# A two-layer Conformer and retention backbone: its opening by channel instead of by token

## The reference

```
mod_x = silu(c) @ ada_w[0] + ada_b[0]          # 6 * 1024 values: shift, scale, gate, twice
mod_c = silu(c_ctx) @ ada_w[0] + ada_b[0]      # the same for the context tokens
h = x * rsqrt(mean(x * x) + eps) * norm1_g     # RMSNorm of each token
h = h * (1 + scale) + shift
z = h @ pw1_w + pw1_b                          # 1024 -> 2048
u = a * sigmoid(g)                             # a, g: the halves of z
u = dwconv(u), 31 taps along the tokens
```

## Time and profile before

| | us |
|---|---|
| median of 3 runs | 1671.44 |
| lowest, highest | 1670.82, 1672.15 |
| the profiled execution | 1671.6 |
| its span | 1669.7 |
| TensorE, matmuls busy | 1641.5 (98%) |
| VectorE busy | 958.0 (57%) |
| ScalarE busy | 677.3 (41%) |
| GpSimd busy | 168.6 (10%) |

### The profile page before, as it was taken

One profiled execution on the slowest core, in us unless ns is written; L12 is line 12 of the kernel. 1 busy time (PEld: TensorE's weight loads), 2 busy tenths in 40 slices (PEclk: granted clock), 3 DMA queues, 4 the chain that ended last, 5 costly groups with the idle time before them and its releaser, 6 DMA issues.

```text
span 1669.7 us, 25661 instructions
## 1 busy us (share of the span) xinstructions
PE 1641.5 (98%) x10040; PEld 1435.3 (86%) x10040; DVE 958.0 (57%) x1511; ACT 677.3 (41%) x1019; POOL 168.6 (10%) x180
## 2 busy tenths in 40 slices
PE   6999989999999999999999999999999999999998
PEld 4777758998888888888899999999999888888888
DVE  6899987763424342334358665656566754543445
ACT  4656667542323222223245333424244543332333
POOL 1488851000000000000000000000000000000000
PEclk9999999999999999999999999999999999999999
DMA  9767742221221212121112121212112323232321
GB/s 338 254 251 251 252 160 95 75 76 48 67 76 56 70 60 67 55 71 57 57 51 92 64 70 39 83 51 63 58 64 76 99 81 123 89 101 89 100 88 51
DMA packets 58062, 165.64 MB, mean 99 GB/s; under 512 B 5288, under 2 KB 7192, under 8 KB 57976
## 3 DMA queue, kind: packets, MB, share of 16 engines
q1 hardware_dynamic: 54120, 150.43, 27.1%
q0 software_dynamic: 2992, 10.88, 2.0%
q10 hardware_dynamic: 864, 3.15, 0.5%
HBM read 162.34 MB, written 2.10 MB: 98 GB/s over the span
## 4 chain that ended last, share of the span: by engine, by line
PE 82%; DVE 14%; ACT 3%; issue 1%; DMA 0%; ACTq 0%; DVEq 0%
PE ps L674 81%; DVE ps L1867 3%; DVE ps L1884 3%; DVE w_lo L1663 2%; DVE rstd L1669 1%; DVE H_lo L1704 1%; PE ps L879 0%; DVE tmp L1692 0%; DVE ps L1882 0%; ACT sq L1251 0%; DVE sq L1692 0%; DVE rstd L1680 0%; ACT tmp L1251 0%; ACT H_hi L1242 0%; DVE ps L1864 0%
## 5 line engine op out<-in xcount | busy, mean ns | idle before, releaser
L674 PE MATMUL ps<-H_hi,w_hi 128*128 128x512 f32 (+1 forms) x1712 | 583.3, 341 | 8.4 <-DVE H_lo L1766 5.1
L674 PE MATMUL ps<-H_lo,w_hi 128*128 128x512 f32 (+1 forms) x1712 | 578.8, 338 | 0.0
L674 PE MATMUL ps<-H_hi,w_lo 128*128 128x512 f32 (+1 forms) x1712 | 578.1, 338 | 0.0
L674 PEld LDWEIGHTS ps<-H_hi,w_hi 128*128 128x128 f32 x1712 | 324.7, 190 | 62.2 <-issue 24.4
L674 PEld LDWEIGHTS ps<-H_hi,w_lo 128*128 128x128 f32 x1712 | 324.8, 190 | 35.0
L674 PEld LDWEIGHTS ps<-H_lo,w_hi 128*128 128x128 f32 x1712 | 324.9, 190 | 34.3
L1663 DVE TENSOR_TENSOR w_lo<-w_raw,w_hi 128x1024 fp32r<-128x1024 f32 x208 | 255.0, 1238 | 107.9 <-ACT w_hi L1204 75.0
L674 PE MATMUL ps<-mid_hi,w_hi 128*128 128x512 f32 (+1 forms) x592 | 199.4, 337 | 0.6
L674 PE MATMUL ps<-mid_lo,w_hi 128*128 128x512 f32 (+1 forms) x592 | 198.4, 335 | 0.0
L674 PE MATMUL ps<-mid_hi,w_lo 128*128 128x512 f32 (+1 forms) x592 | 198.0, 335 | 0.0
L2200 DVE SCALAR_TENSOR_TENSOR tmp<-ps,par,tmp 128x511 f32<-128x511 f32 x66 | 41.6, 658 | 231.3 <-ACT tmp L1548 155.1
(11 more groups left out here) (278 smaller groups left out, 2097.0 us busy)
## 6 DMA issues: line engine op xcount, KB each, us to landing
w_raw<-in_w_units SPq DMA_DIRECT2D x190, 512.0 KB, 3.5
ada<-in_ada_w SPq DMA_DIRECT2D x40, 1024.0 KB, 6.4
w_raw<-in_w_units SPq DMA_DIRECT2D x16, 384.0 KB, 3.3
ada<-in_ada_w POOLq DMA_DIRECT2D x4, 1024.0 KB, 13.1
conv<-in_x ACTq DMA_DIRECT2D x4, 512.0 KB, 5.6
ada_more<-in_ada_w POOLq DMA_DIRECT2D x2, 1024.0 KB, 14.6
conv<-in_ctx ACTq DMA_DIRECT2D x2, 512.0 KB, 9.4
w_raw<-in_w_units POOLq DMA_DIRECT2D x2, 512.0 KB, 18.5
```

What stands on the lines that cost most here:

```text
L674: return nc.tensor.matmul(o, a, b, start=first, stop=last, skip_group_check=True)
```

## The change

The inputs are laid out otherwise on the host (a permutation of the same numbers; no arithmetic): x and the context by channel (`x_cols`), all parameters as one table of 128 rows (`params`), ada_w in groups of contiguous 8 KB per partition (`ada_groups`). In the first layer the columns of the first four groups are interleaved, so that group m carries shift and scale of tiles 2m and 2m+1.

SP loads the parameters, x in four pieces of two tiles, and the identity. The token and parameter transposes and their copies are gone. ScalarE squares each tile, VectorE adds the eight squares (seven adds), and TensorE sums over the partitions with six one-column products. A root of one element, whose result nobody reads, stands before the real one. `keep_busy(n)` makes n products of mean_of with itself into a PSUM bank that is not read: 40 before the sums, 4 behind them, 10 behind the transposes of group 0. The constant group, the modulation and the tiles go by twos, and TensorE's steps alternate between gate and value. Unit 1 is loaded before group 2 instead of behind it.

```diff
-S_XT = 0
-S_PW1 = S_XT + 12
+S_PW1 = 0
...
-FIRST_GROUPS = [0, 2, 1, 3]
+FIRST_GROUPS = 4
...
+        tok_sums = ps[:, 5, 0:6]
+        x_squares = conv[:, KT - 1, 0:TOK]
...
+        def first_shift(j):
+            return 4 * (j // 2) + j % 2
...
+        def x_square(k):
+            return conv[:, k, 0:TOK] if k < KT - 1 else norm_buf[0]
...
-            rows = slice(half * D // 2, (half + 1) * D // 2)
-            g = FIRST_GROUPS[m]
-            eng.dma_start(ada_first[m][half], ada_w[0][rows, g * GROUP * P:(g + 1) * GROUP * P]
-                          .rearrange("(k p) n -> p k n", p=P)).then_inc(ada_first_in[m], 16)
+            eng.dma_start(ada_first[m][half], ada_groups[m, half].rearrange("p (k n) -> p k n", n=GROUP * P)) \
+                .then_inc(ada_first_in[m], 16)
...
-            for n, (lo, rows, src) in enumerate([
-                    (C_COL, 8, c.rearrange("b (t p) -> (b t) p", p=P)),
...
-                r0 = lo % P
-                sp.dma_start(prow[r0:r0 + rows, lo // P, :], src).then_inc(par_rows if lo < DW_W else tap_rows, 16)
-                if n == 0:
-                    sp.dma_start(ident[:], eye).then_inc(eye_in, 16)
+            sp.dma_start(par[:], params).then_inc(par_in, 16)
+            for n in range(KT // 2):
+                sp.dma_start(X[:, 2 * n:2 * n + 2, :], x_cols[:, 2 * n:2 * n + 2, :]).then_inc(x_in[n], 16)
+            sp.dma_start(ident[:], eye).then_inc(eye_in, 16)
...
-            pool.wait_ge(tokens_in[0], 32)
+            pool.wait_ge(x_in[1], 16)
...
             for m in range(2):
                 for half in range(2):
                     load_first(pool, m, half)
-            load_gate_or_value(0)
+                load_gate_or_value(m)
             for half in range(2):
                 load_first(pool, 2, half)
-            load_gate_or_value(1)
...
-            def token_transposes(t):
-                pe.wait_ge(tokens_in[t], 32)
...
-            pe.wait_ge(eye_in, 16)
-            token_transposes(0)
-            token_transposes(1)
...
-            pe.wait_ge(par_rows, 16 * 12)
-            par_transposes([(0, 128), (1, 116)], 6)
-            token_transposes(2)
-            pe.wait_ge(silu_c_ready, 2)
-            pe.wait_ge(par_ready, 1)
-            ada_products(0)
-            pe.wait_ge(tap_rows, 16 * 4)
-            par_transposes([(2, 128), (3, 120), (4, 66), (5, 66)], 1)
-            ada_transposes(0)
-            pe.wait_ge(filled, 4)
+            def keep_busy(n):
+                for _ in range(n):
+                    mm(ps[:, 2, 0:P], mean_of[:], mean_of[:], True, True)
+            pe.wait_ge(filled, 1)
+            keep_busy(40)
+            pe.wait_ge(x_added, KT - 1)
+            for t in range(6):
+                m = mm(tok_sums[:, t:t + 1], x_squares[:, t * P:(t + 1) * P], mean_of[:, 0:1], True, True)
+            m.then_inc(x_summed, 1)
+            keep_busy(4)
             pe.wait_ge(diag_ready, 1)
-            pe.wait_ge(slot_read[1], S_PW1 // 2)
             mm(ps[:, 3, :], mean_of[:], flat_sq[:, LATS], True, True)
             mm(ps[:, 4, 0:CTX], mean_of[:], flat_sq[:, CTXS], True, True).then_inc(rows_ready, 1)
-            ada_products(1)
-            ada_transposes(1)
+            pe.wait_ge(silu_c_ready, 2)
+            ada_products(0)
+            pe.wait_ge(eye_in, 16)
+            ada_transposes(0)
+            keep_busy(10)
...
-            for p in range(2):
-                pe.wait_ge(slot_read[p], S_PW1 // 2)
-            first_block(0, 0, 1)
+            ada_products(1)
+            ada_transposes(1)
+            first_block(0, 0, 2)
             ada_products(2)
-            first_block(0, 1, 3)
+            first_block(1, 0, 2)
             ada_transposes(2)
-            first_block(0, 3, 4)
-            pe.wait_ge(par_ready, 2)
+            first_block(0, 2, 4)
             ada_products(3)
-            first_block(1, 0, 1)
+            first_block(1, 2, 3)
             ada_transposes(3)
-            first_block(1, 1, 4)
-            first_block(0, KT // 2, KT - 2)
+            first_block(1, 3, 4)
+            first_block(0, 4, 6)
+            first_block(1, 4, 6)
+            first_block(0, 6, KT)
             ada_products(4)
-            first_block(0, KT - 2, KT)
-            first_block(1, KT // 2, KT)
+            first_block(1, 6, KT)
             ada_transposes(4)
             ada_products(5)
...
-            for t in range(LT):
-                act.dma_start(xin[:, t, :], x[0, t * P:(t + 1) * P, :]).then_inc(tokens_in[t // 2], 16)
...
-            for s in range(S_PW1):
-                t, jj = s // 4, s % 4
...
-            act.wait_ge(tok_var, 2)
-            A(tok_rstd[:], tok_mv[:, :, 1], ACT.Sqrt, bias=eps[:, 0:1]).then_inc(tok_std, 1)
-            ada_copy(0)
-            ada_copy(1)
-            split_hi(0, 0)
+            act.wait_ge(par_in, 16)
+            for v in range(2):
+                A(silu_c[:, :, v], par[:, C_COL + 8 * v:C_COL + 8 * v + 8], ACT.Silu).then_inc(silu_c_ready, 1)
+            for k in range(KT):
+                act.wait_ge(x_in[k // 2], 16)
+                A(x_square(k), X[:, k, :], ACT.Square).then_inc(x_squared, 1)
+            A(tok_std_row, eps[:, 0:1], ACT.Sqrt)
+            act.wait_ge(x_summed, 1)
+            A(tok_rstd[:], tok_sums, ACT.Sqrt, bias=eps[:, 0:1]).then_inc(tok_std, 1)
             def first_hi(j):
...
-                act.wait_ge(mod_ready, 2 if j < KT // 2 else 4)
+                act.wait_ge(mod_ready, 2 * (j // 2) + 2)
...
-            for j in range(KT // 2):
-                first_hi(j)
-            split_hi(1, 1)
-            ada_copy(2)
-            ada_copy(3)
-            for j in range(KT // 2, KT):
-                first_hi(j)
-                if j in (4, 6):
-                    split_hi(j // 2, j // 2)
+            for m in range(FIRST_GROUPS):
+                if m < 2:
+                    split_hi(m, m)
+                ada_copy(m)
+                for j in (2 * m, 2 * m + 1):
+                    first_hi(j)
+            split_hi(2, 2)
+            split_hi(3, 3)
             ada_copy(4)
...
-            def first_modulation(m, half):
-                dve.wait_ge(mod_sum, m)
-                js = slice(half * GROUP, (half + 1) * GROUP)
+            def first_modulation(m):
+                dve.wait_ge(mod_sum, m + 1)
+                js = slice(2 * m, 2 * m + 2)
                 rows = par[:, ADA_B:ADA_B + 2 * KT].rearrange("p (a j) -> p a j", a=2)[:, :, js]
-                cols = mod[:, 0, 0:2 * KT, :].rearrange("p (a j) c -> p a j c", a=2)[:, :, js, :]
-                v.tensor_tensor(cols, cols, rows.unsqueeze(3).to_broadcast([P, 2, GROUP, 2]), ALU.add).then_inc(mod_ready, 1)
-                dve.wait_ge(mod_ready, 2 * half + 1)
-                v.scalar_tensor_tensor(gain[:, 0, 0, js, :], mod[:, 0, KT + half * GROUP:KT + (half + 1) * GROUP, :], 1.0,
-                                       two(par[:, NORM1 + half * GROUP:NORM1 + (half + 1) * GROUP]), ALU.add, ALU.mult) \
+                cols = mod[:, 0, 4 * m:4 * m + 4, :].rearrange("p (a j) c -> p a j c", a=2)
+                v.tensor_tensor(cols, cols, rows.unsqueeze(3).to_broadcast([P, 2, 2, 2]), ALU.add).then_inc(mod_ready, 1)
+                dve.wait_ge(mod_ready, 2 * m + 1)
+                v.scalar_tensor_tensor(gain[:, 0, 0, js, :], mod[:, 0, 4 * m + 2:4 * m + 4, :], 1.0,
+                                       two(par[:, NORM1 + 2 * m:NORM1 + 2 * m + 2]), ALU.add, ALU.mult) \
                     .then_inc(mod_ready, 1)
-                dve.wait_ge(mod_ready, 2 * half + 2)
+                dve.wait_ge(mod_ready, 2 * m + 2)
...
-            for t in range(6):
-                if t % 2 == 0:
...
+            for k in range(1, KT):
+                dve.wait_ge(x_squared, k + 1)
+                if k > 1:
+                    dve.wait_ge(x_added, k - 1)
+                v.tensor_tensor(x_squares, x_square(0) if k == 1 else x_squares, x_square(k), ALU.add) \
+                    .then_inc(x_added, 1)
+            dve.wait_ge(par_in, 16)
             dve.wait_ge(tok_std, 1)
...
-            dve.wait_ge(par_T, 2)
-            v.tensor_copy(par[:, 256:504], ps[:, 1, 0:248])
-            for layer in range(DEPTH):
-                o = v.tensor_copy(par[:, FFN_DW_W + P * layer:FFN_DW_W + P * layer + 66],
-                                  ps[:, 1, 256 + P * layer:256 + P * layer + 66])
-            o.then_inc(par_ready, 1)
-            ada_sum(0, 0, FIRST_GROUPS[0])
-            for p in range(2):
-                dve.wait_ge(slot_read[p], S_PW1 // 2)
             dve.wait_ge(rows_ready, 1)
             def normed_rows(js):
@@ -1816,20 +1750,19 @@
                     v.tensor_tensor(xn(j), X[:, j, :], rstd_rows, ALU.mult).then_inc(xn_ready, 1)
                 dve.wait_ge(xn_ready, js[-1] + 1)
-            normed_rows(range(KT // 2))
-            dve.wait_ge(par_ready, 2)
-            ada_sum(1, 0, FIRST_GROUPS[1])
-            first_modulation(2, 0)
-            first_shifted(0)
```

(29 more changed lines are left out.)

110 lines of the change are left out of this document (31 added, 79 removed).

## The result

The changed kernel takes **1673.79 us** (median of 20 runs, 1670.83 to 1677.72), the kernel before beside it 1671.21 (20 runs, 1670.33 to 1672.15): ratio 1.0014, 95% interval 1.0008 to 1.0020. It is 2.6 us slower where 4.1 us faster was forecast, and outside the range of 1665.3 to 1670.6. The profiled execution took 1672.88, its span is 1671.1; in the kernel before these were 1671.6 and 1669.7.

What follows compares the result with a forecast made beforehand. VectorE's convolution taps bound the kernel, so only its start on block 0 counts: 20.8 + 32.6 = 53.4 instead of 57.53, 4.1 us earlier, giving 1667.3 us against the median of 1671.44; range 1665.3 to 1670.6.

Steps and rivals of the forecast that it cites:

- Part 1: Opening up to VectorE's first normalising product: loading x by channel and summing squares brings it 3.5 us earlier.
- R: Start of VectorE's first normalising product in the opening: forecast at 20.8 us instead of 24.29.
- the rival with the low clock: Opening on TensorE: low clock doubles sums (+1.2 us) and wide products (+1.5), or order costs waits; 1669.5 us, chance 0.16.
- The rival in which POOL's loads share the engines: Opening loads: x shares DMA engines with POOL's, lands at 14.7 us, gain 2.0, time 1669.4; chance 0.15.
- The slower rival: Opening on TensorE: 40 constant products never raise the clock, take 20 us and delay the sums; 1677.8 us, chance 0.07.
- Part 2: From R to block 0's gates: new order takes 32.6 us against 33.24 before.
- The interleaving: Gate and value steps alternating by twos, from R to block 0's gates: by itself gives only 0.6 us.
- The first step that failed: End of the opening on ScalarE: block 0's sigmoid, with its table load, fits between R+29 and R+31.4, hidden.
- B0: VectorE's start of gate times value on block 0: forecast at R + 32.6, 53.4 us instead of 57.53.
- The step that decides: Behind the opening: later stages keep whatever VectorE's start on block 0 gains, 4.1 us.
- the forecast's own last sign of being wrong: From block 0 through the convolution: a shift at 57 us that is gone by the convolution's end would refute the forecast.
- a group that lands 3 us late: Opening, ada weight loads: late landing cuts the gain to 1.4 to 2.9 us, 1669.5; shared chance 0.16.

Runs made afterwards that it cites:

- e1: Changed kernel with block 0's sigmoid ahead of ScalarE's copy of group 4; 1672.98 us, ratio 1.0011.
- e10c: e9c with 50 constant products ahead of the sums and 8 behind them, in place of 54 and 4; 1668.86 us, ratio 0.9989.
- e3: Changed kernel with 20 more constant products ahead of the products of group 5; 1672.69 us, ratio 1.0011.
- e5: Changed kernel with 54 constant products ahead of the sums in place of 40; 1672.54 us, ratio 1.0006.
- e6: Changed kernel with 54 constant products ahead of the sums and group 4's products two k-steps earlier; 1670.44 us, ratio 0.9994.
- e9c: e7 with one constant sigmoid behind ScalarE's copy of group 4, loading the table ahead; 1670.05 us, ratio 0.9992.
- e7: e6 plus 12 constant products ahead of the LayerNorm's sums and 8 ahead of the second pointwise convolution; 1669.64 us, ratio 0.9992.
- e8: Kernel before the change, with only group 4's products moved late, to where the change put them; 1676.59 us, ratio 1.0031.

## Why the prediction was wrong

*Part 1 was right in its chain, and in its number partly by luck.* R was forecast at 20.8 (the terms as written add up to 20.7) and came at 20.97. The last piece of x ended ScalarE's last wait for a load at 11.72, 0.9 before the 12.6 I took and at the lower bound; but "the earlier six adds keep up" was not quite so: VectorE was still adding, and the last add ended at 14.99 instead of 15.3. The six sums took 1.50 (1.8), the root started at 16.58 (17.1). The 0.5 us gained went back, and 0.2 more, behind the wide products, which took 2.43 at low clock in place of 1.53. That is the wide products' part of the rival with the low clock (0.9 of its 1.5 us); the early x hid it. In the three profiles in which the sums were slow too, R was 22.4 to 22.8. The rival in which POOL's loads share the engines did not come: POOL issued its first at 8.1, and from 8 to 12 us x's queue had 88.8% of the engines' time and POOL's 3.9%. The rule of the Trainium skill on taking turns ("DMA: Bandwidth & Descriptors", Queues, rings and completion order) is not to be seen at the start of POOL's queue, here or in the earlier trace rows. Nor do these rows refute it: from 12 to 13 us x's queue was down to 6.3% and POOL's still at 33.9%, so POOL's queue was slow to start by itself.

*The constant products* ended at 12.87, near the 13 that I gave for a clock that rises soon, and not at the 15.0 of the sum. From 0 to 6 us TensorE has 23 records of them (two to a product) in 4.99 us, 0.22 each, from 6 to 10 us 35 in 4.00, 0.11 each:

```profile
0.00:6.00 6.00, 4.99 (x23) 4.99 (x24) 0.00 (x0) 1.68 (x4) 0.73 (x8) 1.00 0.70 252
6.00:10.00 4.00, 4.00 (x35) 4.00 (x34) 2.13 (x3) 3.33 (x5) 1.88 (x4) 1.00 1.02 416
```

The high level (2.4 GHz) came sooner than for the transposes of the earlier trace rows. The slower rival (the sums held up by the filler) did not come; the filler was too short. Of the five profiles with 40, two have R at 20.9 to 21.0 (filler ended at 12.8 to 12.9) and three at 22.4 to 22.8 (ended by 12.4), so the profile after may flatter the change by over 1 us.

*Part 2 was right up to TensorE's end of the opening.* Transposes 3 ended at R + 21.9 (21.7), the gate's last product was done by 50.22, R + 29.2 (29), VectorE was done at R + 28.5 (28), and transposes 4 started at 54.27. The interleaving gave what was counted for it.

*The first step that failed:* "ScalarE's sigmoid (table 1.28, then 1.1) fits between block 0's end at R+29 and R+31.4". I took the moved products of group 4 as 1.86 us of TensorE and left out who copies them. ScalarE's copy of group 4 stands ahead of the sigmoid in its own order, waited for these products until 52.21, and pushed the sigmoid to 54.12. B0 came at R + 34.2 instead of R + 32.6. e1, with the copy behind the sigmoid, gives 1.3 us of it back; e10c, with the sigmoid's table loaded ahead, 1.1.

*The step that decides:* "Whatever that start gains, the stages behind it keep." B0 came 2.3 us early, by B1 that was gone, and B2 was late by 1.8: the forecast's own last sign of being wrong, "a shift at 57 us that is gone by the end of the convolution". I read the earlier trace rows for VectorE's 19.82 alone; the same row has TensorE's matmuls busy 20.00 of 20. TensorE has 0.5 us of slack in a block, so its lateness in block 0 is VectorE's lateness in block 2. And that lateness came from a step that I had moved in the order and costed only on TensorE: group 4's products stood 4.05 us ahead of transposes 4, behind which group 5 is wanted, over one buffer, and group 5's loads took 4.9 and 7.4 us to land. In time these products stayed where they were, at 50.2, and so did the loads; only what wants the loads moved forward. I named "a group that lands 3 us late" among the rivals, priced it as a smaller gain, 1669.5, and gave that whole rival 0.16. It missed the clock that falls behind the wait (about 2 us by e3) and, above all, that TensorE and VectorE can't work it off.

*The sum, corrected.* Against the kernel before at B2: -3.3 for R, +1.0 for B0 - R (34.23 against 33.24), then +2.4 for B0 to B1 (24.53 against 22.16) and +1.8 for B1 to B2 (24.14 against 22.37): +1.8, which is what B2 shows (103.87 against 102.06). The rest took 0.5 less, and the spans differ by 1.4. The medians differ by 2.6. That the profiled run has an early R could account for the other 1.2, but only profiles show R, so this is not shown.

*What stays open.* Why the clock fell at about 18 us in e5, e6, e9c and e10c, behind idle times of at most 1.5 us, and not in e7 was not settled; nor what the 2.4 to 4.0 us outside the span are in some runs of e7, e9c and e10c; nor was it tried to give group 5 a second buffer, which would take the wait away in the change's own order. And that the two groups of the changed kernel's runs are those with and without low clock behind the wait for group 5 is argued from one profile of each kind and from the mean clock of the runs (0.996 or 0.997 up to 1671.8 us, 0.993 or 0.994 from 1674.4 on; in e8 0.997 or 0.998 up to 1675.2, and 0.994 to 0.996 from 1676.4 on), not shown run by run.

## What to carry to other kernels

When a step is moved, cost it at every engine it passes through, and again at its buffer: a product needs a copy on another engine, and frees the room into which the next load must go. In a stage in which the bounding engine is busy 99%, look whether a second engine is at 98%: then a gain at the entry lasts only as far as that second engine is not late. And constant products that are to keep a clock up must reach up to the work that they are for: 40, of which 16 had been counted at the low level's duration, ended 2 to 4 us short here, and 54 reached it. That helped the sums right behind them; at the wide products the clock was low all the same in four of the five profiles with 50 or 54.
